# Gates through a half tangent, norms folded into the projections, and the first layer's column sums dealt out anew

## The reference

```python
hx = rmsnorm(x, g_pre[layer]) * (1.0 + scale_x) + shift_x
...
y_x = (o_x.reshape(b, n, A_WIDTH) * jax.nn.silu(gate_x)) @ w_out
...
x = x + gate_x * rmsnorm(yx, g_post[layer])
...
q = jax.nn.silu(causal_conv(q, conv_q)).reshape(B, S, N_HEADS, HEAD_DIM)
merged = jax.nn.sigmoid(ga) * y_a + jax.nn.sigmoid(gb) * y_b
...
hid = jax.nn.silu(xb @ w_gate[e]) * (xb @ w_up[e])
```

## Time and profile before

| | |
|---|---|
| median of 3 runs | 2142.73 us |
| profiled execution | 2140.6 us |
| its span, first to last instruction | 2138.7 us |
| busy share: TensorE, VectorE, ScalarE, GpSimd | 90%, 49%, 19%, 3% |
| mean granted TensorE clock | 0.954 of full |
| HBM read | 359.88 MB |

### The profile page before, as it was taken

The page is one execution under the profiler, slowest core; times in us unless marked ns, Lnnn a source line. Parts: engine busy times, 40 slices in busy tenths (PEclk is TensorE's granted clock), DMA queues, the critical chain, the costliest instruction groups (busy, mean ns, idle before and its releaser), DMA issues. The chain is left out here.

```text
span 2138.7 us, 19056 instructions
## 1 busy us (share of the span) xinstructions
PE 1914.4 (90%) x7154; PEld 1008.8 (47%) x7154; DVE 1047.0 (49%) x2190; ACT 412.6 (19%) x1025; POOL 69.0 (3%) x54
## 2 busy tenths in 40 slices
PE   3998699899788899998988999797994999999996
PEld 1544255444454444443344665485863443444442
DVE  2485754578685466566645335346743222212222
ACT  1221043200473222211113123111100111111111
POOL 0000001000000000002520000000000000000000
PEclk8999899999999999999999999898996999999998
DMA  8323500254100233331012231233363799999992
GB/s 357 138 79 138 210 7 0 82 196 177 60 1 1 102 119 137 138 118 39 25 40 79 88 129 40 94 117 128 119 275 133 316 428 427 427 426 428 428 427 102
DMA packets 30377, 362.19 MB, mean 169 GB/s; under 512 B 3499, under 2 KB 3660, under 8 KB 5964
## 3 DMA queue, kind: packets, MB, share of 16 engines
q1 hardware_dynamic: 30284, 360.94, 42.4%
HBM read 359.88 MB, written 1.05 MB: 169 GB/s over the span
## 5 line engine op out<-in xcount | busy, mean ns | idle before, releaser
L694 PE MATMUL bank<-hT,slot 128*128 128x256 f32 (+1 forms) x832 | 266.2, 479 | 0.0
L694 PEld LDWEIGHTS bank<-hT,slot 128*128 128x128 f32 x832 | 158.4, 191 | 101.5 <-issue 89.4
L345 DVE SCALAR_TENSOR_TENSOR product<-slot,cond_rows 128x1024 f32<-128x1024 f32 x160 | 195.5, 1222 | 16.1 <-DMA slot<-panels_dram 9.8
L2366 PE MATMUL bank<-slot,hmT 128*64 128x512 f32 x496 | 174.3, 592 | 1.2 <-ACT hmT L2421 1.2
L1464 PE MATMUL bank<-hT,slot 128*128 128x512 f32 x384 | 171.7, 601 | 1.9 <-PEq L213 1.9
L515 PE MATMUL bank<-slot,gT 128*128 128x512 f32 x384 | 166.7, 593 | 3.6 <-PEq L213 3.6
L2366 PE MATMUL bank<-late_slots,hmT 128*64 128x512 f32 x432 | 139.5, 592 | 0.0
L2462 DVE TENSOR_SCALAR hT<-hT 128x512 f32<-128x512 f32 x16 | 6.8, 427 | 261.4 <-ACT hT L2428 261.4
L515 PEld LDWEIGHTS bank<-slot,gT 128*128 128x128 f32 x384 | 72.2, 190 | 92.1 <-issue 92.1
L1464 PEld LDWEIGHTS bank<-hT,slot 128*128 128x128 f32 x384 | 72.3, 193 | 85.0 <-issue 85.0
L2366 PEld LDWEIGHTS bank<-slot,hmT 128*64 128x64 f32 x496 | 55.4, 137 | 87.5 <-issue 86.2
(11 more groups left out here) (367 smaller groups left out, 2653.7 us busy)
## 6 DMA issues: line engine op xcount, KB each, us to landing
slot<-panels_dram SPq DMA_DIRECT2D x91, 2048.0 KB, 10.5
late_slots<-panels_dram SPq DMA_DIRECT2D x40, 2048.0 KB, 19.6
slot<-panels_dram SPq DMA_DIRECT2D x40, 1024.0 KB, 5.2
branch_slot<-panels_dram SPq DMA_DIRECT2D x9, 2048.0 KB, 21.9
mod_slot<-panels_dram SPq DMA_DIRECT2D x4, 2048.0 KB, 18.4
slot<-panels_dram SPq DMA_DIRECT2D x4, 1536.0 KB, 6.5
slot<-panels_dram SPq DMA_DIRECT2D x2, 1280.0 KB, 19.8
x_tok<-tokens_dram SPq DMA_DIRECT2D x4, 512.0 KB, 10.7
```

Of the source, the lines that this page charges most:

```text
L345: last = m.nc.vector.scalar_tensor_tensor(out=m.product[:], in0=m.slot(panel)[:, c * D:(c + 1) * D], scalar=1.0, in1=m.cond_rows[:, s, :], ...
L694: last = self.m.nc.tensor.matmul(self.bank(g), self.m.slot(panel)[:, k * width + j * P:k * width + (j + 1) * P], self.m.hT[:, k, 0:self.n] ...
L2366: last = nc.tensor.matmul(ps[6 + kind][a * SLOTS:(a + 1) * SLOTS, :], xs[:, k, a * SLOTS:(a + 1) * SLOTS], m.slot(expert_panel(pair, kind, ...
```

## The change

- Gates: ScalarE forms tanh(x/2) in place of exp(-x). The silu becomes one VectorE instruction, (tanh + 1) * x, twice the silu; the factor 0.5 goes into the instruction that later multiplies with it (in `attention`, in `conv_gate`; 0.25 for query times key in `mlstm_heads`). The sigmoid in `second_inputs` is one tensor_scalar; in `mlstm_heads` ScalarE writes the tangent straight to its place and `second_merge` adds 1 in the instruction that multiplies (the result is doubled, and `project_out` halves it). Add, reciprocal and multiplication of lines 708 to 713, 1961 to 1963 and 2462 to 2464 are gone.
- `second_inputs`: the silu is done channel tile by channel tile between the convolutions.
- Entry: the tokens are normed and turned between the modulation products; scale and shift are applied afterwards in place, on VectorE and ScalarE, in eight instructions each of 128 x 256. `rows` is issued ahead of the weight panels, and the first weight panel (`a_cq0`) ahead of the two column panels.
- `project_out`: `ready` per half; squares, root, norm and turning are done per tile inside the block; `norm_to_channels` is gone, and so is the block that loads `g_ffn`, which is now issued at the start of `project_out`.
- Column sums of layer 0: 32 in front of the norm of the latents, 20 between the gates (2 each for the first four, then 3), 12 in `latent_qkv` (4 at its start, 4 behind each half of the queries), none beside the values. SyncE's list is changed to match.

The diff, cut to its core and moved left by eight columns:

```diff
@@ enter_first @@
     sp.dma_start(m.rows[:], m.dram["rows"]).then_inc(rows_landed.sem, rows_landed.sixteen())
+    m.issue(sp, m.index("a_cq0"))
+    for n in range(2):
+        m.issue(sp, m.index("column0.8") + n)
+    m.issue(sp, m.index("a_ckv0"))
+    m.issue(sp, m.index("a_gate0.0"))
     sp.wait_ge(rows_landed.sem, rows_landed.at(16))
...
+    def turn_tokens(t):
+        pe.wait_ge(normed_ready.sem, normed_ready.at(t + 1))
+        for half in range(2):
+            if t >= 2:
+                taken = by_act if half else by_dve
+                pe.wait_ge(taken.sem, taken.at(t - 1))
+            for k in range(4):
+                last = nc.tensor.transpose(token_bank(t, half)[:, k * P:(k + 1) * P],
+                                           normed[:, t, (4 * half + k) * P:(4 * half + k + 1) * P], m.ident[:, :])
+            last.then_inc(turned.sem, turned.one())
...
+    product(0)
+    pe.wait_ge(rows_taken.sem, rows_taken.at(4))
+    turn_tokens(0)
+    turn_tokens(1)
+    product(1)
+    turn_tokens(2)
+    turn_tokens(3)
+    product(2)
+    turn_columns(0)
+    product(3)
+    turn_columns(1)
...
+    for t in range(NT):
+        act.wait_ge(turned.sem, turned.at(2 * t + 2))
+        nc.scalar.activation(m.hT[:, 4:8, t * P:(t + 1) * P],
+                             token_bank(t, 1)[:, :].rearrange("p (k t) -> p k t", k=4), ACT.Copy) \
+            .then_inc(by_act.sem, by_act.one())
+    act.wait_ge(by_act.sem, by_act.at(NT))
+    act.wait_ge(modulation.sem, modulation.at(1))
+    for s in range(2):
+        for k in range(4, 8):
+            own_part = m.hT[:, k, s * N:(s + 1) * N]
+            nc.scalar.activation(own_part, own_part, ACT.Identity, scale=m.scale1[:, s, k:k + 1],
+                                 bias=m.shift[:, s, k:k + 1])
...
+    for t in range(NT):
+        nc.vector.tensor_scalar(normed[:, t, :], m.x[:, t, :], m.rstd[:, NORM + t:NORM + t + 1], None, ALU.mult) \
+            .then_inc(normed_ready.sem, normed_ready.one())
+    take_turned(0)
+    take_turned(1)
+    take_chunk(1)
+    take_turned(2)
+    take_turned(3)
+    take_chunk(2)
+    take_columns(0)
+    take_chunk(3)
+    take_columns(1)
...
+    nc.vector.nop().then_inc(modulation.sem, modulation.one())
+    dve.wait_ge(by_dve.sem, by_dve.at(NT))
+    for s in range(2):
+        for k in range(4):
+            own_part = m.hT[:, k, s * N:(s + 1) * N]
+            nc.vector.tensor_scalar(own_part, own_part, m.scale1[:, s, k:k + 1], m.shift[:, s, k:k + 1],
+                                    ALU.mult, ALU.add)
...
@@ Gates @@
-    def exponential(self, act, g):
+    def half_tangent(self, act, g, out=None):
+
+
 act.wait_ge(self.ready.sem, self.ready.at(g + 1))
+if out is not None:
+    self.m.nc.scalar.activation(out, self.bank(g), ACT.Tanh, scale=0.5).then_inc(self.done.sem, self.done.one())
+    return
...
-
-    def finish(self, dve, g, out, silu):
-nc, chain, t = self.m.nc, self.m.sig("dve_chain"), self.tmp[:, g % 2, 0:self.n]
-dve.wait_ge(self.exp.sem, self.exp.at(g + 1))
-after(dve, nc.vector.tensor_scalar(t, t, 1.0, None, ALU.add), chain)
-if silu:
-    after(dve, nc.vector.reciprocal(t, t), chain)
-    last = nc.vector.tensor_tensor(out, self.bank(g), t, ALU.mult)
-else:
-    last = nc.vector.reciprocal(out, t)
-last.then_inc(self.done.sem, self.done.one())
+self.m.nc.scalar.activation(self.tmp[:, g % 2, 0:self.n], self.bank(g), ACT.Tanh, scale=0.5) \
+    .then_inc(self.tangent.sem, self.tangent.one())
+
+    def doubled_silu(self, dve, g, out):
+dve.wait_ge(self.tangent.sem, self.tangent.at(g + 1))
+self.m.nc.vector.scalar_tensor_tensor(out=out, in0=self.tmp[:, g % 2, 0:self.n], scalar=1.0, in1=self.bank(g),
+                                      op0=ALU.add, op1=ALU.mult).then_inc(self.done.sem, self.done.one())
+
...
@@ project_out @@
+    if by_token is not None:
+        sp.dma_start(by_token[1], m.dram["g_ffn"]).then_inc(gain_landed.sem, gain_landed.sixteen())
+        m.issue(sp, N_DENSE + EXPERT_SLOTS.index(BRANCH_SLOT))
+    for n, i in enumerate(panels):
+        sp.wait_ge(ready.sem, ready.at(2 * (NX - 1) + n + 1))
         m.load_next(sp, i)
...
+    for t in range(NX):
+        turn(t)
...
+        for n in range(2):
+            act.wait_ge(added.sem, added.at(2 * t + n + 1))
+            nc.scalar.activation(m.scratch[:, 0, n * 512:(n + 1) * 512], m.x[:, t, n * 512:(n + 1) * 512], ACT.Square,
+                                 accum_out=m.sums[:, NORM + 2 * n + t:NORM + 2 * n + t + 1]) \
+                .then_inc(squares_x.sem, squares_x.one())
+        act.wait_ge(squares_x.sem, squares_x.at(2 * t + 2))
...
+            for n in range(2):
+                dve.wait_ge(squares.sem, squares.at(2 * t + n + 1))
+                nc.vector.tensor_tensor(y[:, halves[n]], bank(t, n)[:, :], m.gate[:, t // NX, halves[n]], ALU.mult)
+            after(dve, nc.vector.tensor_tensor(m.sums[:, one], m.sums[:, one], m.sums[:, NT + t:NT + t + 1], ALU.add),
+                  chain)
             inverse_root(m, dve, m.sums[:, one], 1.0 / D, m.var[:, one], m.rstd[:, one], m.tmp[:, one])
+            for n in range(2):
+                nc.vector.scalar_tensor_tensor(out=m.x[:, t, halves[n]], in0=y[:, halves[n]], scalar=m.rstd[:, one],
+                                               in1=m.x[:, t, halves[n]], op0=ALU.mult, op1=ALU.add) \
+                    .then_inc(added.sem, added.one())
...
+                last = nc.vector.scalar_tensor_tensor(out=normed[:, t, halves[n]], in0=m.x[:, t, halves[n]],
+                                                      scalar=m.rstd[:, x_one], in1=by_token[1][:, halves[n]],
+                                                      op0=ALU.mult, op1=ALU.mult)
+            last.then_inc(normed_ready.sem, normed_ready.one())
+    for t in range(NX):
+        take_turned(t)
...
@@ latent_layer, latent_inputs @@
-    if layer == 0:
-norm_to_channels(m, NT, m.hT, lambda s, k: m.scale1[:, s, k:k + 1], lambda s, k: m.shift[:, s, k:k + 1])
...
         if columns:
-            columns.refill(sp, 2 * n)
-            columns.refill(sp, 2 * n + 1)
+            for i in (range(0, 5), range(5, 8))[n]:
+                columns.refill(sp, i)
         sp.wait_ge(ready.sem, ready.at(tq + n * NT))
         m.load_next(sp, panels[n])
     for n in range(2):
+        if columns:
+            for i in ((8,), (9, 10, 11))[n]:
+                columns.refill(sp, i)
         sp.wait_ge(gates.ready.sem, gates.ready.at(4 * n + 4))
         m.load_next(sp, panels[2 + n])
-        if columns:
-            for i in ((4, 5), (6,))[n]:
-                columns.refill(sp, i)
...
         columns.some(dve, 16)
         columns.all_taken(dve, 4)
         gate_columns(m, dve, layer)
+        columns.some(dve, 16)
...
-        gates.finish(dve, g, m.gT[:, g, 0:tq * P], True)
+        gates.doubled_silu(dve, g, m.gT[:, g, 0:tq * P])
         if columns:
-            columns.some(dve, 1 if g < 4 else 2)
+            columns.some(dve, 2 if g < 4 else 3)
...
@@ latent_qkv @@
     if columns:
-        columns.refill(sp, 7)
+        columns.refill(sp, 12)
+        columns.refill(sp, 13)
...
         if columns:
-            for i in ((8, 9), (10, 11, 12), (13, 14, 15))[n]:
+            for i in ((14,), (15,), ())[n]:
                 columns.refill(sp, i)
...
+    if columns:
+        columns.some(dve, 4)
...
-            if columns:
-                columns.some(dve, 2)
-    if columns:
-        columns.some(dve, 10)
+        if columns:
+            columns.some(dve, 4)
...
-            if columns:
-                columns.some(dve, 1)
...
@@ second_inputs @@
+silu_after = {(2, 1): (0, 1), (2, 2): (2,), (2, 3): (3,), (3, 0): (4, 5), (3, 1): (6, 7)}
...
-    act.wait_ge(conved.sem, conved.at(2 * M_H))
-    nc.scalar.activation(expo[:], qkT[:], ACT.Exp, scale=-1.0).then_inc(expd.sem, expd.one())
+        for c in silu_after.get((n, j), ()):
+            act.wait_ge(conved.sem, conved.at(c + 1))
+            nc.scalar.activation(tangent[:, c, :], qkT[:, c, :], ACT.Tanh, scale=0.5).then_inc(tangents.sem, tangents.one())
...
+        if j >= 2:
+            silu(j - 2)
...
-    dve.wait_ge(expd.sem, expd.at(1))
-    after(dve, nc.vector.tensor_scalar(expo[:], expo[:], 1.0, None, ALU.add), chain)
-    after(dve, nc.vector.reciprocal(expo[:], expo[:]), chain)
-    nc.vector.tensor_tensor(qkT[:], qkT[:], expo[:], ALU.mult)
+    for c in (2 * M_H - 2, 2 * M_H - 1):
+        silu(c)
     for g in range(4):
-        gates.finish(dve, g, go[:, g, :], False)
+        gates.sigmoid(dve, g, go[:, g, :])
...
@@ mlstm_heads @@
-                gates.exponential(act, g)
+                out, j = gate_tiles[g]
+                gates.half_tangent(act, g, out[:, j, :])
...
-            for g in range(PER_UNIT * (step - 1), PER_UNIT * step):
-                out, j = gate_tiles[g]
-                gates.finish(dve, g, out[:, j, :], False)
...
@@ expert_lists @@
-        dve.wait_ge(expd.sem, expd.at(pair + 1))
```

(5 more changed lines are left out.)

284 lines of the change are left out of this document (127 added, 157 removed).

## The result

The changed kernel took 2059.58 us (median of 4 runs, 2059.05 to 2061.14), the kernel before 2143.03 in the same session: a ratio of 0.9613, 95% interval 0.9596 to 0.963. The forecast was 2062 us. The profiled execution took 2061.1 us, its span is 2059.4.

The account below looks back on a forecast made before the run. TensorE, busy 90% of the span, was taken as the bound, so its idle stretches were the only cheap time. Terms 27.4 + 17.9 + 10.5 + 24.7 = 80.5 us off 2140.6 gave 2060.1, as a median 2062 us; range 2050 to 2076.

Parts of the forecast that it names:

- Gates, layers 1 to 3: Only the last gate tile's chain is in the open: -3.8, -3.8, -2.0 us; clock behind layers 2 and 3 -2.4, -1.7.
- the experts: Expert stage, where DMA share is 1.00 and VectorE has slack: cheaper gates bring 0, still 28.5 us a pair.
- second_inputs: Silu done tile by tile lies beside the convolutions but for the last: idle 13.07 to 1.2, -11.9 us, clock -1.8.
- a_out3: Last layer's projection back: shorter chain for the last tile before the mixer's first product, -4.7 us.
- s_out: Projection back before the routing: per-tile norm, gain row loaded early; routing product at 1622.0 against 1635.16, -13.2 us.
- Entry: Up to layer 0's first product: early norm, rows issued first; 44.5 against 57.76, -13.3 us, clock gives back 2.8: -10.5.
- Column sums: Layer 0, sums moved to other places: latent_inputs -1.8 us, latent_qkv and first attention products -22.9 (-21.4 and -1.5), together -24.7.
- More from the clock: Rival: fewer idles keep TensorE at 2.4 GHz longer, 6 to 12 us more, 2052 us; chance 0.12.
- Entry and sums half as good: Rival: entry brings 5 and column sums 12; 2080 us, halves of it 2073; chance 0.16.
- Tanh in another table: Rival: tanh and exp need separate ScalarE table loads, +20.5 us in the heads and some elsewhere, 2085 us; chance 0.06.
- Column panels late: Rival: VectorE bound by column panel refills in layer 0, 2154 us, slower than before from 7.7 us a panel; chance 0.02.
- layer 0's inputs: Stretch from layer 0's first product to its heads: +1.0 us, from clock +2.8 and sums -1.8.

Follow-up runs that it names:

- e3: Changed kernel with the old gate chain (exp, add, reciprocal, multiply) in the first seven of eight gate tiles of the first-block layers: 2066.05 us.
- e4: Changed kernel with the old gate chain in only the last of the eight gate tiles of each first-block layer: 2076.27 us.
- e5: Changed kernel with the silu of the expert pairs by the old chain (exp, add 1, reciprocal, multiply): 2060.63 us.
- e6: Changed kernel with all eight tangents and silu instructions of second_inputs in one row behind the last convolution: 2059.13 us.
- e9: Changed kernel plus unread transposes in TensorE's idle stretches in project_out (54 and 26) and at the routing (56): 2055.68 us.
- e8: Changed kernel with the 20 column sums between the gates dealt 3, 3, 3, 3, 3, 3, 2, 0 and one refill one wait earlier: 2055.80 us.
- e10: Changed kernel plus unread transposes in TensorE's idle at the entry's end (34) and before the last tile's turning in layers 0 to 2 (32): 2055.55 us.
- e1: Changed kernel with layer 0's column sums and SyncE's refills dealt out as in the kernel before: 2078.37 us.
- e11: Changed kernel with the unread transposes of e9 and e10 and the gate sums dealt as in e8, all in one: 2043.65 us.
- e12: e11 with fewer unread transposes, 16 in place of 32 in layers 0 to 2 and 50 in place of 56 at the routing: 2045.85 us.
- e7: Changed kernel with the small constant rows issued behind the five weight panels again, as before: 2066.47 us.

## Why the prediction was right, point by point

- **Gates, layers 1 to 3.** Right in place and size: idles of 3.82, 1.74, 1.26 for 3.5, 1.8, 1.3. That only the last tile's chain counts is shown by e3 and e4; the clock behind layers 2 and 3 measured 2.1 and 1.7 for 2.4 and 1.7. That the experts gain nothing is shown by e5.
- **`second_inputs`.** Size right, -11.4 for -11.9; the reason half wrong. "Done tile by tile it lies beside the convolutions but for the last" is true and makes no difference: by e6 the shorter chain alone does it. I had not compared the new silu's length, 3.4 us, with what TensorE still has to do behind the convolutions, and had overlooked the four old gates that made 7.8 of the 13.07 us.
- **`a_out3`.** -4.9 for -4.7, the chain of short instructions as summed. No run puts the old order of `project_out` back, neither here nor in `s_out`: these two terms, 16 us together, are read off the timelines.
- **`s_out`.** The term most off, -11.3 for -13.2. The projection itself gave 12.8: from the last addition (1548.29) to the routing product it is 7.6 us for 7.3 forecast. The last turning took more than I had put down: behind an idle of 3.79 the eight transposes took 1.97, at half clock, and in e9, with that idle filled, the stage is 0.65 shorter. Most of the 12.8 is the block that waited for the gain row:

```profile
1629.15 2.48 DVE L647 SCALAR_TENSOR_TENSOR gate_rows_all<-x_tok,rstd 128x1024 f32<-128x1024 f32 x2 [9.34 <-PEq L213]
```

VectorE stood 9.34 us before this norm in the old kernel. Now the row is issued at 1520.51, lands 15.1 later, and is wanted at 1538.39: in time by under 3 us. The other part of the miss, 1.5, is in the merge: some 3.4 us near its start were at half clock. Among the profiled executions those of e5 to e8 and e10 had it too (17.0 us), those of e1 to e4, e9, e11 and e12 not (15.4), with the same code there. In e1 to e4 the idle before it was 0.91 us, but in e9, e11 and e12 it was 1.26 as in the slower ones. What decides it stays open.

- **Entry.** TensorE's written order gave 39.6 for the 38.9 of my sum; ScalarE's eight in-place instructions took 4.04 for 3.6 (VectorE's 2.67); and the clock took back 2.6 for 2.8, which e10 shows to be the idle's doing. `rows` landed at 30.5, as worked out, and e7 shows that 5.2 of the 12.7 hang on this; that the rest is the early norm's was not tested by itself. The Trainium skill, "DMA: Bandwidth & Descriptors", section "Two DMAs through the same engine are not ordered", gives no order in which transfers end; in these runs a transfer of 62 KB behind 7 MB took 36.9 and 37.4 us, and 24.9 issued sooner. So the trace doesn't speak against that page, as the prediction had it: the page denies an order to rely on, and says nothing against one that is seen.
- **Column sums.** -21.4 and -1.5, to the tenth of a us. The slack in front of the norm of the latents was smaller than reckoned (sums done at 91.2, read at 93.4; I had 84 and 88), because of the wait of 4.33 and because a sum with the reading of its accumulator takes 1.27, not 1.22; but it was there. By e1 this term is the change's own: 19.0 of the stretch go when the deal goes. The idle before the heads fell by 3.0 (8.55 to 5.53) for the 2.4 forecast.
- **The rivals.** More from the clock: in part. TensorE's busy time fell by 9.2 us, where the forecast's clock terms were a net 4; that is 5.2 beyond them, just short of the rival's 6 to 12, and the idle time fell by as much less than the rest of the forecast. Entry and sums half as good: no (halves of its 18.2 would be 2071, not the 2073 of the prediction). Tanh in another table: the changed kernel has five table loads of 1283 ns, as before. As the Trainium skill, "ScalarE: Activation LUTs", section "Table sets: the hidden batching unit", has it, tanh and exp stand in one set; its other line, ln with exp in one load, is not what the two loads in `second_inputs` show, which are there still. Column panels late: one wait of 4.33 us, far from 7.7 for each.

The mechanism was right in all large terms but the reason given for `second_inputs`. That the sum is this close is in part luck. The span fell by 79.3 for 80.5, with steps off by up to 1.9 us that partly cancel: `s_out`, the entry and the experts one way, layer 0's inputs (-1.5) and the routing (-0.8) the other. The median is 2.4 under the forecast because it lies 1.6 below the profiled execution now, and lay 2.1 above it before.

## What to carry to other kernels

Where one engine is busy 90% of the span, list its idle stretches and ask of each what chain ends it: what stands behind the last product of a stage is worth shortening, and 60 us of faster elementwise work elsewhere bring nothing (e5) or, where VectorE has slack, go unseen (layers 1 to 3 in e3; in layer 0, where it had too little, 6 us came out). Look at who waits for the waiter: TensorE's row named a copy on VectorE, and that one stood behind a transfer. And issue small things that a block waits for ahead of large ones (5.2 us in e7).

## What was not expected of the hardware

- An idle of TensorE can cost twice, itself and the half clock behind it, and the second can be bought off with work that nobody reads: 34 transposes in the entry's idle of 5.4 us took 2.6 us off the next stretch in e10 (of which 1.1 came back in the stretch behind) and 2.4 in e11 against e8, with nothing given back there. In the layers, with an idle of 4.85 us, it brought less: 32 transposes ended too late in two of three, and 16 brought the half clock back (0.64 over the first 4.7 us).
- An edit of a few us moves the low stretches of the clock on products far away: +1.9 us in untouched stages of e8, 1.7 us at the merge present or absent. A single profiled span is therefore no better than 2 us for such edits; stretches at the edit are.
